# A gated projection moved ahead of the linear attention's products, and an eleventh buffer for the expert stream

## What is computed

```python
u = rmsnorm(x1)                       # x1: output of the first block
dq, dk, dv, gq, gk, gv, gg, gr = split(u @ w_in_2)
da  = differential attention of dq, dk, dv          # 4 heads, chunks of 64
og  = chunked gated linear attention of gq, gk, gv  # decay from gr
x2  = x1 + concat(rmsnorm(da), rmsnorm(og) * silu(gg)) @ w_o_2
x3  = x2 + cross_attention(x2, mem_2)               # keys, values: rmsnorm(mem_2) @ w_ckv_2
out = x3 + sum over the 2 chosen of 32 experts of gate * (silu(x @ Wg) * (x @ Wu)) @ Wd
```

## Time and profile before

| | |
|---|---|
| median of 3 runs | 1137.18 us (1136.93 to 1137.8) |
| profiled execution, its own time | 1140.0 us |
| its span | 1137.7 us |
| PE busy | 931.5 us (82%), mean granted clock 0.921 |
| weight loads of PE | 585.4 us (51%) |
| DVE, ACT, POOL busy | 403.1, 170.2, 243.2 us |
| read from HBM | 288.51 MB, 255 GB/s over the span |
| chain that ended last | PE 61%, DMA 27%, DVE 6%, ACT 2%, SP queue 2% |

### The profile page before, as it was taken

One profiled execution on the slowest core, in us unless ns is written; L12 is line 12 of the kernel. 1 busy time (PEld: TensorE's weight loads), 2 busy tenths in 40 slices (PEclk: granted clock), 3 DMA queues, 4 the chain that ended last, 5 costly groups with the idle time before them and its releaser, 6 DMA issues.

```text
span 1137.7 us, 12449 instructions
## 1 busy us (share of the span) xinstructions
PE 931.5 (82%) x5006; PEld 585.4 (51%) x5006; DVE 403.1 (35%) x984; ACT 170.2 (15%) x370; POOL 243.2 (21%) x368
## 2 busy tenths in 40 slices
PE   7999999999999899699999999665656566574837
PEld 3775487789999778575544554221221212131312
DVE  5537834752234827655545524110010101010101
ACT  2113232530001022022312312000000000000000
POOL 4444132043844849630000000000000000000000
PEclk9999999999999999899999999887787878697879
DMA  7636232233545255234228358999999999999997
GB/s 278 199 116 219 96 126 75 75 104 126 195 169 185 77 189 182 74 138 154 78 74 318 131 215 357 429 428 427 429 426 428 427 428 427 430 427 428 428 421 277
DMA packets 64312, 290.38 MB, mean 255 GB/s; under 512 B 9015, under 2 KB 11902, under 8 KB 52222
## 3 DMA queue, kind: packets, MB, share of 16 engines
q1 hardware_dynamic: 63966, 289.04, 64.4%
q10 hardware_dynamic: 288, 0.52, 0.1%
HBM read 288.51 MB, written 1.05 MB: 255 GB/s over the span
## 4 chain that ended last, share of the span: by engine, by line
PE 61%; DMA 27%; DVE 6%; ACT 2%; SPq 2%; issue 1%; ACTq 0%; DVEq 0%
PE ACC L520 11%; PE ACC L661 10%; PE ACC L535 8%; PE AUX L1050 7%; PE ACC L658 7%; DMA ring<-in_w_e_gate_dram 5%; DMA ring<-in_w_e_down_dram 5%; PE ACC L559 5%; DMA SQE<-in_w_e_up_dram 3%; DMA BIG<-in_w_e_up_dram 3%; DMA PJ<-in_w_e_up_dram 3%; DMA PJ<-in_w_e_down_dram 3%; DMA BIG<-in_w_e_gate_dram 3%; PE AUX L1086 2%; PE ACC L942 2%; DMA SQE<-in_w_e_gate_dram 2%
## 5 line engine op out<-in xcount | busy, mean ns | idle before, releaser
L1282 POOL TENSOR_TENSOR ring<-ring 128x256 f32<-128x256 f32 x272 | 200.5, 767 | 190.2 <-PE ACC L661 75.6
L1050 PE MATMUL AUX<-ring,R 128*32 128x512 f32 x416 | 115.9, 721 | 55.0 <-DMA BIG<-in_w_e_up_dram 20.3
L535 PE MATMUL ACC<-BIG,ring 128*128 128x256 f32 (+1 forms) x464 | 106.2, 382 | 0.0
L535 PEld LDWEIGHTS ACC<-BIG,ring 128*128 128x128 f32 (+1 forms) x464 | 84.6, 187 | 15.6 <-issue 3.6
L2282 DVE SCALAR_TENSOR_TENSOR R<-R,AUX 128x512 f32<-128x512 f32 x8 | 5.5, 688 | 233.8 <-ACT R L1660 233.8
L1050 PE MATMUL AUX<-R 128*32 128x512 f32 x112 | 62.9, 726 | 23.3 <-DMA ring<-in_w_e_gate_dram 13.1
L1050 PE MATMUL AUX<-BIG,R 128*32 128x512 f32 x192 | 54.9, 736 | 28.8 <-DMA PJ<-in_w_e_up_dram 21.1
L1050 PEld LDWEIGHTS AUX<-ring,R 128*32 128x32 f32 x416 | 28.6, 129 | 94.7 <-issue 94.7
L520 PE MATMUL ACC<-ring,BIG 128*128 128x512 f32 (+2 forms) x192 | 75.9, 554 | 0.0
L1050 PE MATMUL AUX<-PJ,R 128*32 128x512 f32 x192 | 53.7, 722 | 17.6 <-DMA ring<-in_w_e_up_dram 10.5
L1086 PE MATMUL AUX<-ring,BIG 128*32 128x512 f32 x192 | 52.3, 705 | 13.8 <-DMA BIG<-in_w_e_down_dram 7.4
(11 more groups left out here) (345 smaller groups left out, 1425.0 us busy)
## 6 DMA issues: line engine op xcount, KB each, us to landing
ring<-in_w_in_dram SPq DMA_DIRECT2D x20, 2048.0 KB, 7.8
ring<-in_w_e_gate_dram SPq DMA_DIRECT2D x14, 2048.0 KB, 27.7
ring<-in_w_e_up_dram SPq DMA_DIRECT2D x12, 2048.0 KB, 29.8
ring<-in_w_e_down_dram SPq DMA_DIRECT2D x10, 2048.0 KB, 29.4
BIG<-in_w_e_up_dram SPq DMA_DIRECT2D x8, 2048.0 KB, 32.5
PJ<-in_w_e_gate_dram SPq DMA_DIRECT2D x6, 2048.0 KB, 26.6
BIG<-in_w_e_down_dram SPq DMA_DIRECT2D x6, 2048.0 KB, 29.0
PJ<-in_w_e_down_dram SPq DMA_DIRECT2D x6, 2048.0 KB, 35.2
```

Source lines behind the costliest of these rows:

```text
L535: mm = nc.tensor.matmul(bank[0:m, j * S:(j + 1) * S], w[:, i, a + j * P:a + j * P + m], rhs[:, i, :], start=(i == 0), stop=(i == k - 1))
L1050: mm = nc.tensor.matmul(bank[r, :], M_xt[:, k, r], w[e][:, k, :], start=(k == 0), stop=(k == KD - 1))
L1282: ins = g.tensor_tensor(out[:, k, :], a[:, k, :], b[:, k, :], op)
```

## The change

In the middle of the second block, PE's program has the projection gg right behind ckv1, then `kend`, then `intra` and the turned heads; the three states are made inside dv, after its fourth matmul. DVE combines gv whole before `norm_heads`, and combines ckv1 inside it. ACT takes the tanh of gg before the drains of the turned heads. At the block's start the block sums of the memory rows come earlier, the memory's scale (an `rsqrt`) later, and the squares of the rows no longer wait for it. R1 and R2 become one tensor, R12, which is stream buffer 4; what stood there for the experts moves to R4, GB and BIG2, the routing tables into the masks' tensor, and the output is staged in PJ. POOL's program and its order stay.

```diff
-STREAM = 10
+STREAM = 11
...
-        R1 = sb("R1", TT * D)
-        R2 = sb("R2", KD * S)
+        R12 = sb("R12", TT * D + KD * S)
+        R1, R2 = R12[:, 0:TT * D], R12[:, TT * D:]
...
-        RT = R4[:, 512:1184]
+        RT = MASKS
...
-        M_xt = kt(R1[:, 0:1024], KD)
-        M_o, M_gated, M_hid = R2[:, 0:1024], R2[:, 1024:1536], R2[:, 1536:2048]
+        X3T = kt(BIG2[:, 1280:3328], KD)
+        M_xt = kt(R4[:, 512:1536], KD)
+        M_o, M_gated, M_hid = GB[:, 0:1024], GB[:, 0:512], GB[:, 512:1024]
...
-        OUT = v2(R1)
+        OUT = v2(PJ)
...
-        stream = [slots[4], slots[5]] + [slots[slot_no[chunk_at[name]]] for name in ("wcq0", "wcq1")] + spare[0:2] + [
+        stream = [slots[4], slots[5]] + [slots[slot_no[chunk_at[name]]] for name in ("wcq0", "wcq1")] + [R12[:, :]] + spare[0:2] + [
...
             project_blocks("ckv1", R2T, T_mem2, mem2_sums)
+            project_blocks("gg", XT3, T_x, x1_sums)
             pe.wait_ge(gla_products, 1)
             pe.wait_ge(gla_padded, 1)
+            bank, full = aux(3, "kend")
+            for t in range(TT):
+                for h in range(2):
+                    mm = nc.tensor.transpose(bank[:, (2 * t + h) * P:(2 * t + h + 1) * P], KE[:, h, t * P:(t + 1) * P],
+                                             ident[:, :])
+            mm.then_inc(full, 1)
...
-            project_blocks("gg", XT3, T_x, x1_sums)
-            wait_drained(pe, "kend")
-            wait_drained(pe, "gv")
-            for c in range(3):
+            def make_states():
+                wait_drained(pe, "kend")
+                wait_drained(pe, "gv")
+                for c in range(3):
...
-            project("dv", XT3, between=finish_gla)
+            project("dv", XT3, between=finish_gla, after=lambda done, total: make_states() if done == 4 else None)
...
                         elif n == 4:
+                            for t in range(TT):
+                                for h in range(2):
+                                    wait_full(sp, ("xk", t, h))
+                                    wait_full(sp, ("xq", t, h))
+                        elif n == 5:
                             wait_full(sp, ("S", first_unit["C"] + 3))
                             wait_full(sp, ("T", first_unit["C"] + 3))
-                        elif n in (6, 7):
-                            sp.wait_ge(x3_done, n - 4)
+                        elif n in (7, 8):
+                            sp.wait_ge(x3_done, n - 5)
                         elif n == 9:
+                            wait_full(sp, ("router", 1))
+                        elif n == 10:
                             wait_full(sp, ("x3", 1, 1))
                             sp.wait_ge(rows_scaled, 2)
...
             square_rows(2, v2(XT), R3v, [(mem2_landed, 16)])
+            square_rows(3, X3, ZTv, [(x_added, 2)], col=76)
             act.wait_ge(mem2_scaled, 1)
-            square_rows(3, X3, ZTv, [(x_added, 2)])
...
+            act.wait_ge(gla_products, 1)
+            act.wait_ge(gla_padded, 1)
+            wait_drained(act, "gg")
+            a_.activation(R3[:, 0:1024], GG.rearrange("p t n -> p (t n)"), ACT.Tanh, scale=0.5).then_inc(tanh_ready, 1)
             act.wait_ge(pads_cleared, 5)
...
                 if h == 0:
-                    dve.wait_ge(rows_squared, 4)
-                    rsqrt(2, SMALL[:, 64:66], SMALL[:, 78:80]).then_inc(mem2_scaled, 1)
-            row_sums(T_mem2, quarters(R2T), mem2_sums)
-
-            norm_rows(3, X3, ZTv, 5)
+                    row_sums(T_mem2, quarters(R2T), mem2_sums)
+
+            norm_rows(3, X3, ZTv, 5, col=76)
...
             combine("ckv0", by_rows(R1v, 0), range(2, 4))
+            rsqrt(2, SMALL[:, 64:66], SMALL[:, 78:80]).then_inc(mem2_scaled, 1)
...
-            combine("gv", by_rows(GV), range(1))
+            combine("gv", by_rows(GV))
 
             def apply_d():
-                combine("gv", by_rows(GV), range(1, 2))
-                scale_heads(hv(DQ[:, 0, :], 8), 0, 8)
-                scale_heads(hv(DK[:, 0, :], 8), 16, 8)
-                combine("gv", by_rows(GV), range(2, 4))
-                scale_heads(hv(DQ[:, 1, :], 8), 8, 8)
-                link(scale_heads(hv(DK[:, 1, :], 8), 24, 8))
+                combine("ckv1", by_rows(R1v, 512))
+                for t in range(TT):
+                    scale_heads(hv(DQ[:, t, :], 8), 8 * t, 8)
+                    ins = scale_heads(hv(DK[:, t, :], 8), 16 + 8 * t, 8)
+                link(ins)
...
             norm_heads(SQ[:, :], 32, 64, apply_d, 2)
-            combine("ckv1", by_rows(R1v, 512))
+            combine("gg", by_rows(GG))
             link(v.memset(ATT, 0.0))
+
+            bank = wait_full(dve, "kend")
+            kb_ = bank[:, :].rearrange("p (n d) -> p n d", n=4)
+            v.tensor_copy(KEN[0:64, 0, :, :], kb_[0:64])
+            v.tensor_copy(KEN[64:128, 1, :, :], kb_[64:128]).then_inc(free_sem("kend"), 1)
```

More of the change, by code:

```diff
@@ L174, in two_block_layer @@
         R_le, R_rest, R_rank = rt(152, TT, 32), rt(216, TT, 32), rt(280, TT, 32)
[L175 to L178, removed]
+        R_exp = rt(344, TT, 37)
+        R_dif = NW[:, 0:TT * 37].rearrange("p (t n) -> p t n", t=TT)
+        R_den, R_full = rt(418, TT), rt(420, 1)
+        R_gate, R_over = rt(424, TT, 32), rt(488, TT, 32)
+        SELH = rt(552, TT, 16).bitcast(BF16)
         R_rs = SMALL[:, 76:78]
[L182 to L183 removed]
+        X3T = kt(BIG2[:, 1280:3328], KD)
+        M_xt = kt(R4[:, 512:1536], KD)
+        M_o, M_gated, M_hid = GB[:, 0:1024], GB[:, 0:512], GB[:, 512:1024]
         M_hidt, M_place = kt(R3[:, 0:512], 4), R3[:, 512:768]
@@ L846, in _ @@
                 turn(2 + t, ("dk", t))
[L847 to L852, removed]
-            project_blocks("gg", XT3, T_x, x1_sums)
-            wait_drained(pe, "kend")
-            wait_drained(pe, "gv")
-            for c in range(3):
[L857 to L861, removed]
+            def make_states():
+                wait_drained(pe, "kend")
+                wait_drained(pe, "gv")
+                for c in range(3):
+                    bank, full = aux(c, ("state", c))
+                    for h in range(2):
+                        mm = nc.tensor.matmul(bank[:, h * 256:(h + 1) * 256], KEN[:, c % 2, 2 * (c // 2) + h, :],
+                                              GV[:, c // 2, h * 256:(h + 1) * 256], start=True, stop=True)
+                    mm.then_inc(full, 1)
             def finish_gla():
@@ L954, in score_experts @@
                         wait_drained(pe, ("x3", t, i // 4))
-                    mm = nc.tensor.matmul(bank[:, 0:36], R2T[:, i, t * P:(t + 1) * P], WR3[:, i, :],
+                    mm = nc.tensor.matmul(bank[:, 0:36], X3T[:, i, t * P:(t + 1) * P], WR3[:, i, :],
                                           start=(i == 0), stop=(i == KD - 1))
@@ L1193, in _ @@
                                 for i in range(2):
+                                    m = STREAM + i
+                                    src = (WG, WU, WD)[m // GROUP % 3][m // (3 * GROUP) * GROUP + m % GROUP]
                                     c = slice(h * SLOT // 2, (h + 1) * SLOT // 2)
-                                    sp.dma_start(stream[i][:, c], WD[(STREAM + i) % GROUP].rearrange("(p k) n -> p (k n)", p=P)[:, c]).then_inc(
+                                    sp.dma_start(stream[i][:, c], src.rearrange("(p k) n -> p (k n)", p=P)[:, c]).then_inc(
                                         moe_landed[i], 16)
@@ L1381, in link, with square_rows @@
                 act.wait_ge(act_steps, steps[0])
-            def square_rows(n, src, junk, ready, tiles=range(TT)):
+            def square_rows(n, src, junk, ready, tiles=range(TT), col=64):
                 for r in ready:
@@ L1712, in rsqrt, with norm_rows @@
                     link(ins)
-            def norm_rows(n, src, dst, squared):
+            def norm_rows(n, src, dst, squared, col=64):
                 dve.wait_ge(rows_squared, squared)
-                rsqrt(2, SMALL[:, 64:66])
+                rsqrt(2, SMALL[:, col:col + 2])
                 for t in range(TT):
@@ L2112, in _ @@
                                   pb[:, 1]).then_inc(free_sem(("intra", t)), 1)
-            bank = wait_full(dve, "kend")
-            kb_ = bank[:, :].rearrange("p (n d) -> p n d", n=4)
-            v.tensor_copy(KEN[0:64, 0, :, :], kb_[0:64])
-            v.tensor_copy(KEN[64:128, 1, :, :], kb_[64:128]).then_inc(free_sem("kend"), 1)
-            combine("gg", by_rows(GG))
             for c in range(3):
```

19 lines of the change are left out of this document (7 added, 12 removed).

## The result

| | before | after |
|---|---|---|
| median of the runs | 1137.06 us (4 runs, 1136.47 to 1137.8) | 1124.16 us (4 runs, 1123.87 to 1124.3) |
| profiled execution: own time, span | 1140.0, 1137.7 us | 1124.19, 1122.3 us |
| mean granted clock | 0.921 | 0.927 |

The ratio is 0.9886 (95% interval 0.9869 to 0.9903): faster by 12.9 us. The forecast was 1117.8, with a range from 1113.5 to 1124.0. The sign was right; the time lies 6.4 us above the forecast and 0.16 outside the range.

The account below looks back on a forecast made before the run. PE's work bound it before slice 26, expert transfers after. Middle 11.8, start 1.0 + 1.7 and buffer 4.9 sum to 19.4 us: profiled 1140.0 becomes 1120.6, less 2.8 to the median 1117.8; range 1113.5 to 1124.0.

Parts of the forecast that it names:

- ckv1's stall: Middle stretch: PE's 8.66 us wait for DVE between gv and ckv1 goes, and with it 2.9 of lower clock in ckv1.
- the wait ahead of `kend`: Middle stretch: `kend` waits 3.7 us for its bank, 1.3 of it used by turned groups; the remaining 2.3 goes.
- POOL is what is late next: Middle stretch: POOL's sums come late for gg, whose four waits are 0, 0.9, 1.3 and 1.3, 3.5 us in all.
- The buffer: Expert stream: an eleventh buffer puts everything one load further at each gate, worth 4.9 us (bounds 0 and 4.9).
- rival 1: Expert stream: the buffer brings nothing because something other than transfers holds the stream; 1122.7 us, chance 0.05.
- Rivals 2, 4 and 5: 2: wait behind dv, 1123.7, chance 0.07; 4: clock stays down, 1149.6, 0.03; 5: gg waits on POOL, buffer hidden, 1137.2, 0.02.
- rival 3: Middle stretch: the clock falls in gg and comes back after the turned heads, +9.2, so 1127.0 us; chance 0.05.
- gg's sums, each 4 additions of 0.75: POOL in the middle stretch: each sum for gg takes 3.0 us, so PE's waits in gg total 3.5.
- the 0.3 in ckv1: Middle stretch: w12 is ready at 468.5 to 468.9 against 468.4, so ckv1 loses 0.3 us waiting for POOL.
- kend with gg ... another 1.7 at the lower clock: Middle stretch: `kend` with gg took 14.3 where full clock gives 12.5; this 1.7 us was counted as lost time to win.
- the 1.7 lost in 398 to 403 is taken as won too: Block's start: with the remaining wait at 1.9, the clock stays up, winning 1.7 us (bounds 0 and 1.7).
- I take 1.0 us: Block's start: the rows' `rsqrt` starts at 390.0, shortening PE's 2.88 us wait by 1.0 us (bounds 0 and 2.9).

Follow-up runs that it names:

- experiments 2 and 4: 2: the changed kernel without the eleventh stream buffer, 1128.42 us; 4: the changed kernel with the old order at the block's start, 1124.81 us.
- experiment 6: The changed kernel with DVE's combine gg ahead of the eight scale and gain instructions of the heads: 1125.48 us, ratio to before 0.9892.
- Experiment 8: The changed kernel with the eight scale and gain instructions of dq and dk left out: 1119.95 us, ratio to before 0.9844.
- Experiment 1: The kernel before, unedited, profiled once more: 1135.91 us, span 1134.1.
- experiment 3: The changed kernel with the old order from gv to dv on PE, ACT and DVE: 1131.46 us, ratio to before 0.9947.

## Why the prediction was right in sign and wrong in size

**Right.** The main step held: ckv1's stall is gone, and the clock that it cost with it (ckv1 12.25); so is the wait ahead of `kend`; POOL is what is late next, from the second of gg's sums on in experiments 2 and 4, as written, and from the first in the changed kernel's own profile; states and turned heads cost nothing behind dv. The buffer brought 4.3 by the runs and about 5 by the profiles, where 4.9 were forecast, and the transfers still set the end, so rival 1 is out. Rivals 2, 4 and 5 did not come: dv starts 10.07 us earlier (497.95 with the states' 2.59 counted ahead of it, against 505.43 + 2.59) and ends 10.07 earlier (518.00 against 528.07), so nothing is given back in it, and the result is faster. Of rival 3 a trace is there. In the changed kernel's profiled execution the granted clock was 0.79 in 478 to 486, behind waits of 1.58 and 2.53; in experiments 2 and 4, which run the same middle and have waits of 2.25 and 1.68, it was 1.00 in that stretch, and gg took 16.6 in both, 2.2 less, of which 1.7 is the clock. In experiment 6 it was 0.72 in 492 to 498, behind waits of 1.57, 0.97 and 0.96. So waits of this size can bring the clock down, and don't always. The loss was 1.7, not the 9.2 of that rival.

**Wrong, in three terms.** Two of the signs named for the profile show it too: gg ended at 489.6, where about 485 was forecast, and the last product of dv at 518.0, where it was 513.

1. *"gg's sums, each 4 additions of 0.75"*, and from it the 3.5 us of waits. I took 0.71 and 0.80 as the bounds, from rows in which POOL worked beside a quiet DVE or beside mixed work. But the change itself moves DVE's eight scale instructions next to these additions: I had DVE at combine ckv1 until 472.3 and POOL's sums from 472.3, and did not lay the two queues side by side. Beside the scales one addition takes 1.1. From ckv1's start to dv's start the working gives 30.0 + 0.3 + 3.5 = 33.8; experiments 2 and 4 show 35.7 (457.47 to 493.16, and 459.31 to 494.98). That is 1.9 us. Experiment 8, which has no such neighbours, takes 32.3 (457.77 to 490.07), so the collision costs 3.4. An error the other way hid 1.6 of it, which was luck. The description of the kernel and the prediction both say that product 5 needs w12. The code says product 6; the third number of each entry is the sum of W that it waits for:

```python
products = [(w11, x[0][0], 0, 0), (w12, x[1][0], 0, 0), (S_a, T[:, 0], 1, 1), (S_b, T[:, 1], 2, 2),
            (w21, T[:, 2], 3, 3), (w22, T[:, 3], 0, 4), (w12, x[1][1], 4, 0)]
```

   So the 0.3 in ckv1 and the last 1.3 of gg's waits could not come. In experiment 8 products 4 and 5 run in one piece from 479.06 to 482.75, and w12 is ready only at 481.81 (470.48 + 11.33). With this put right the working gives 33.8 - 1.6 = 32.2, next to the 32.3 of experiment 8.

   A wait that I had put at 0 to 0.4, gg's first for combine ckv1, is in the 35.7 too, with 1.1 (1.07 in experiment 8), but it is absent in the changed kernel's profile. The last of the `rsqrt`'s twelve small instructions makes the difference, beside the first of POOL's three products. I had priced it as in the kernel before, 0.65, where POOL made additions at that time. First DVE and POOL in experiment 8, then DVE in the changed kernel, where POOL's product (467.45) and it start together:

```profile
466.81 1.31 DVE L1719 SCALAR_TENSOR_TENSOR RS<-NW 128x32 f32<-128x32 f32 x1
466.80 1.27 POOL L1368 TENSOR_TENSOR PJ<-BIG 128x512 f32<-128x512 f32 x1
```

```profile
467.46 0.19 DVE L1719 SCALAR_TENSOR_TENSOR RS<-NW 128x32 f32<-128x32 f32 x1
```

2. *"kend with gg ... another 1.7 at the lower clock"*, part of the 2.9 of ckv1, and at the start *"the 1.7 lost in 398 to 403 is taken as won too"*. These were losses of one execution, which stood 2.8 above the median; they are enough to explain that excess. Experiment 1 has the same waits and neither fall. In the middle 45.6 shrinks to 43.0, 2.6 us; at the start 1.7 us go. (1.7 of the 2.6 is the fall behind `kend`'s wait, the rest the cheaper fall in ckv1.) I counted them as gains of the change against the profiled 1140.0, and then took the 2.8 off once more to come to the median, though the changed kernel cannot win against the median what the median never lost. With experiment 1 as the measure the forecast was 2.6 + 1.7 = 4.3 us too low by this; that execution stood 1.2 below the median, so against a usual one it may be about 3.
3. *"I take 1.0 us"* for the earlier `rsqrt` at the start: 0.66. It starts at 391.03, not 390.0, because ACT's squares ended later, and the slow pace of the small instructions lasted until 395.7.

The account, an estimate: 19.4 - 1.9 - 4.3 - 0.3 = 12.9 us, which is what was measured; and for the middle by itself 43.0 - 35.7 = 7.3, as experiment 3 found. That it closes to a tenth is luck in part. Its base is experiment 1, 1.2 below the median, and its 35.7 is that of experiments 2 and 4, where the changed kernel's own profile has 36.8 (458.41 to 495.20), 1.7 of clock more and 0.6 of waits less; the two nearly cancel. Profile against profile is firmer: the span went from 1137.7 to 1122.3, 15.4 us, 4.0 short of the 19.4. The middle is 3.0 short (45.6 became 36.8, 8.8 and not 11.8), the start 1.5 (gv ends 1.2 earlier, not 2.7), and behind dv it is 0.4 better than forecast. The excess of 2.8 came on top, taken off a profile whose counterpart after the change had none (1124.19, with a median of 1124.16).

The range failed at its high end for both reasons: its least gain of 13.8 kept all of the middle's clock terms in and was then taken from the median, and its bound for gg had no row of POOL and DVE at once.

## What to carry to other kernels

When a change moves work on one engine, write down what each *other* engine does in the same microseconds after the move, and price both from rows where they overlap, not from rows where one was quiet. Separate a wait, which every execution has, from what the clock did after it, which one execution may have and the next not: look at a second profile before a clock term goes into a sum, and never subtract a profile's excess over the median when the terms of the sum are already made of it. Read from the code, not from memory, which operand each product waits for: here one product's difference hid half of a collision. And when POOL gates TensorE, order its queue by who is waiting, and give ACT what DVE would do with two inputs in SBUF.

## What the runs showed of the hardware

**DVE and POOL slow each other.** A POOL addition of 128x256 takes 0.71 alone or beside `combine` (11.33 for 16) and 1.1 beside DVE's 128x512 products with both inputs in SBUF, which go from 0.63 to 1.0 to 1.1 in the same stretch (4.10 to 4.59 for four, against 2.50). `combine`, whose instructions nearly all have an input in PSUM, stays at 0.42 and costs POOL nothing. While the two run side by side, one pair takes 9.06 / 8 = 1.13 us, where one after the other would be 0.71 + 0.63 = 1.34. Small instructions pay more for their size: those of the `rsqrt` mostly take 0.65 beside POOL's additions, and 0.16 to 0.17 when POOL is idle, the ones with a single input in SBUF and a constant too (L1707 at 392.21 in the changed kernel, 0.65), and the last of them 1.31 in experiment 8 beside a product of 1.27.

The Trainium skill, page "SBUF — State Buffer", section "SBUF: two separate sides", says that a DVE instruction with two SBUF inputs and a GpSimd operation that reads SBUF share a pair of ports as an exclusive lock, held for the whole instruction, so that the other blocks. By that rule the pair would take the full 1.34; the trace agrees that the scales collide with the additions and on most of the price, and shows about 0.2 us of overlap per pair. Weighed against the move of the scales, the rule would have put the collision into the sum.

**The same wait, two clocks.** Behind 2.88 us of idleness of TensorE the granted clock was 0.76 in 397 to 404 in one execution, and behind 2.89 us it was 1.00 in two others (experiments 1 and 4, sixteen turns in 1.97 each). Behind the 2.38 ahead of `kend` it was 0.91 in 486 to 492 in that one execution, and 1.00 in experiments 1 and 3. Behind 8.7 us it was 0.50 in 466 to 470 in all three profiles that have the wait. What decides between the two in the shorter waits stays open; no run here was made to tell it.
